# Four adaLN tiles behind each product weight, and the last silu ahead of the root, in a two-block Trainium2 kernel

## What is computed

```python
mod = silu(c) @ mod_w + mod_b                # shift, scale, gate
h = rmsnorm(x, norm_g) * (1 + scale) + shift
cv, cg, cs, lx, ls = split(h @ w_in)         # five parts of 1024
v = conv31(cv * sigmoid(cg)); v = silu(layernorm(v)) @ pw2_w + pw2_b
y_conv = v * silu(cs)
xs = conv4(lx)                               # 8 heads of 128
r = sigmoid(xs @ wr + br); i = sigmoid(xs @ wi + bi)
a = exp(-8 * r * softplus(-lam)); bx = sqrt(1 - a**2) * i * xs
y_lru = scan(a, bx) * silu(ls)
x = x + (1 + gate) * (concat(y_conv, y_lru) @ w_out)
# second block: adaLN from silu(c_2) @ ada_w_2 and silu(c_ctx_2) @ ada_w_2,
# then an mLSTM mixer and a convolutional FFN
```

## Time and profile before

| | |
|---|---|
| median of 3 runs | 2344.55 us (2343.93 to 2348.63) |
| the profiled execution | 2347.46 us |
| its span, first to last instruction | 2345.6 us |
| mean granted TensorE clock | 0.951 |
| PE busy | 2157.1 us, 92% |
| DVE busy | 1103.7 us, 47% |
| ACT busy | 774.6 us, 33% |
| POOL busy | 671.8 us, 29% |

### The profile page before, as it was taken

One profiled execution on the slowest core, in us unless ns is written; L12 is line 12 of the kernel. 1 busy time (PEld: TensorE's weight loads), 2 busy tenths in 40 slices (PEclk: granted clock), 3 DMA queues, 4 the chain that ended last, 5 costly groups with the idle time before them and its releaser, 6 DMA issues.

```text
span 2345.6 us, 26000 instructions
## 1 busy us (share of the span) xinstructions
PE 2157.1 (92%) x9876; PEld 1785.9 (76%) x9876; DVE 1103.7 (47%) x1039; ACT 774.6 (33%) x884; POOL 671.8 (29%) x308
## 2 busy tenths in 40 slices
PE   5999799997999999999979957979999999999995
PEld 4788687876878787888859946747888888887874
DVE  7689988777333656412236652082222222412124
ACT  4333254564342332122334443232222222302122
POOL 1466455544222221211201124402222222222240
PEclk7999999999999999999989977979999999999997
DMA  9431111221212333356578852121112122123211
GB/s 364 169 128 45 30 59 60 64 68 45 72 59 79 123 90 120 104 172 212 171 200 235 224 200 85 54 72 54 45 45 80 57 77 80 54 72 117 67 59 72
DMA packets 280109, 245.19 MB, mean 105 GB/s; under 512 B 7714, under 2 KB 251523, under 8 KB 280035
## 3 DMA queue, kind: packets, MB, share of 16 engines
q1 hardware_dynamic: 270355, 234.75, 32.5%
q10 hardware_dynamic: 9680, 9.44, 1.2%
HBM read 196.12 MB, written 48.04 MB: 104 GB/s over the span
## 4 chain that ended last, share of the span: by engine, by line
PE 41%; issue 38%; DVE 10%; POOL 6%; DMA 3%; ACT 2%; SPq 0%; POOLq 0%; ACTq 0%; DVEq 0%
PE PS L1372 31%; POOL wl L678 5%; DVE PS L1835 5%; PE PS L1641 1%; PE PS L1649 1%; PE PS L1642 1%; PE PS L1675 1%; PE PS L1528 1%; DVE SCR L1749 1%; DMA B<-rows_d 1%; PE PS L1615 1%; DMA SCR<-in_ctx 1%; PE PS L1635 1%; PE PS L1621 1%; PE PS L1634 1%
## 5 line engine op out<-in xcount | busy, mean ns | idle before, releaser
L1372 PE MATMUL PS<-XH,wh 128*128 128x512 f32 x2448 | 762.9, 393 | 28.9 <-POOL wl L678 18.3
L678 POOL TENSOR_TENSOR wl<-raw,wh 128x1024 fp32r<-128x1024 f32 (+2 forms) x177 | 415.6, 2348 | 1248.0 <-ACT wh L865 1026.1
L1372 PE MATMUL PS<-XL,wh 128*128 128x512 f32 x2448 | 759.1, 391 | 0.0
L1372 PE MATMUL PS<-XH,wl 128*128 128x512 f32 x2448 | 758.4, 391 | 0.0
L1372 PEld LDWEIGHTS PS<-XH,wh 128*128 128x128 f32 x2448 | 460.9, 189 | 133.3 <-POOL wl L678 16.3
L1372 PEld LDWEIGHTS PS<-XL,wh 128*128 128x128 f32 x2448 | 462.5, 189 | 96.9
L1372 PEld LDWEIGHTS PS<-XH,wl 128*128 128x128 f32 x2448 | 462.4, 189 | 96.9
L1835 DVE SCALAR_TENSOR_TENSOR PS<-B,PJ,PS 128x1022 f32<-128x1022 f32 (+7 forms) x197 | 251.1, 1274 | 7.5
L865 ACT ACTIVATE wh<-raw 128x1024 fp32r<-128x1024 f32 (+1 forms) x120 | 125.4, 1045 | 312.4 <-PE PS L1372 245.8
L2246 DVE SCALAR_TENSOR_TENSOR SCR<-SCR,PV 128x1008 f32<-128x1008 f32 x22 | 28.0, 1271 | 256.6 <-ACT SCR L1308 256.6
L939 ACT ACTIVATE wh<-raw 128x1024 fp32r<-128x1024 f32 (+1 forms) x56 | 54.1, 965 | 268.5 <-PE PS L1372 232.8
(11 more groups left out here) (337 smaller groups left out, 2440.7 us busy)
## 6 DMA issues: line engine op xcount, KB each, us to landing
B<-in_ada_w SPq DMA_DIRECT2D x48, 512.0 KB, 6.0
raw<-in_ffn_up_w SPq DMA_DIRECT2D x44, 512.0 KB, 4.1
raw<-in_w_in SPq DMA_DIRECT2D x40, 512.0 KB, 3.8
raw<-in_m_in_w SPq DMA_DIRECT2D x29, 512.0 KB, 5.2
proj_d<-B SPq DMA_DIRECT2D x17, 512.0 KB, 3.0
mod_tiles<-in_mod_w SPq DMA_DIRECT2D x16, 512.0 KB, 13.0
raw<-in_w_out SPq DMA_DIRECT2D x16, 512.0 KB, 4.3
B<-proj_d SPq DMA_DIRECT2D x8, 1024.0 KB, 6.5
```

Of the source, the lines that this page charges most:

```text
L678: tt(wl[slot][:, 0:kc, :], raw[slot][:, 0:kc, :], wh[slot][:, 0:kc, :].bitcast(F32), ALU.subtract).then_inc(lo_done, 1)
L1372: last = mm(ps[:, c:c + step_n], W[:, k, :], Y[:, k, c:c + step_n], start=(seen == 0), stop=(seen == total - 1))
```

## The change

SyncE's loop of the first pass loads four adaLN tiles behind each unit of weights from unit 4 on, not three: 3 to 6 behind unit 4, and so on to 19 to 22 behind unit 8 and tile 23 behind unit 9. On ScalarE, for the last head, a silu of one column (`spare` from `eps`) is added behind the copy of line 1050, and `ls_evac` of the last head goes ahead of the cast of G1's second unit, of three high halves and of the root. Its former place, between the high halves of blocks 6 and 7, is empty. All else is as before.

```diff
         eps = sb("eps", [P, 1])
+        spare = sb("spare", [P, 1])
...
             for U in range(4, 2 * KD):
                 l1_load(U)
-                for n in range(3 * (U - 3), min(3 * (U - 2), (1 + EARLY) * KD)):
+                for n in range(3 + 4 * (U - 4), min(3 + 4 * (U - 3), (1 + EARLY) * KD)):
                     ada_load(n)
...
                 f(r_t, r_t, ACT.Copy, bias=1.0).then_inc(ev("th_ok"), 1)
                 if last:
+                    f(spare[:], eps[:], ACT.Silu)
+                    ls_evac(i)
                     hi(ls_unit(i) + 2)
                     for k in range(DVE_HIGH, KD - 2):
                         lru_high(k)
...
             lru_high(KD - 2)
-            ls_evac(KD - 1)
             lru_high(KD - 1)
```

## The result

Five executions of the changed kernel gave a median of **2334.15 us** (2332.66 to 2335.51), beside 2346.96 us (2343.93 to 2348.63) for five of the kernel before: ratio **0.9948, 95% interval 0.9934 to 0.9963** (8.7 to 15.5 us). It is faster by 12.8 us where 21.2 were forecast, and its time lies above the forecast range. The profiled execution took 2335.51 us with a span of 2333.7. The changed kernel has one line more from line 171 on, up to three more near line 1053 and two behind it: 939 and 995 are now 940 and 996, the root of 1056 is 1059, and 1372, 1499, 1528, 1829 and 1852 are 1374, 1501, 1530, 1831 and 1854.

A forecast was written before the change was run, and what follows sets the result against it. TensorE, busy 92% of the span, bounds the kernel; two waits, 11.7 and 10.2 us, can be removed. Gains of 13.7 + 7.5 = 21.2 us take 2347.46 to 2326.3, median 2323.4; range 2320 to 2329.

The forecast's parts named there:

- the second part: ScalarE's last silu ahead of the root lets TensorE start G1 near 558.6, not 567.06, ending its opening 7.5 us earlier.
- Block 6: In G1's opening, its low half is ready at 570.3; ten TensorE blocks, 13.7 us, then end at 584.0.
- block 7's later root: In G1's opening, block ready at 576.1, TensorE comes at 578.5: the delay costs nothing, 2.4 us of cover.
- the Trainium skill's drain: On ScalarE, about 1.38 us more per table switch, 2.66 in all; would cut 1.4 us, but not charged.
- The adaLN sums: On VectorE, last sum ends at 140.0 instead of 151.99, set by tile 23's late load; VectorE gains 12.0 us.
- part 1: Four adaLN tiles behind each weight: gate products of head 0 end 14.5 us earlier, 0.8 given back, worth 13.7 us.
- The first taps: VectorE's four first conv taps before the short conv, 9.2 us in all, taken as unchanged; bounds 4.0 earlier, 3.9 later.
- the margin: At head 0's gate products, xs's low half is ready at 280.8, TensorE arrives at 281.17: 0.4 us to spare.
- part 1 falls short: Rival: bad tap collisions or slower landings leave 1 to 3.5 us of wait at the gates; 2324.4 to 2327, chance 0.12.
- half clock in the sparse stretch: Rival: TensorE's clock falls inside G1's opening, 556.9 to 571.7, costing 2.4 us; 2325.8, chance 0.12.
- Both gains stay: Behind G1's opening, all is set by TensorE's products and what follows them, so the full 21.2 us reaches the end.
- The base: Profiled execution of the kernel before, 2347.46 us, lies 2.9 above the median of three runs; 2326.3 becomes 2323.4.

The follow-up runs named there:

- f4_noload: The changed kernel without the added one-column silu, so the table load stands at the real silu: 2333.81 us, ratio 0.9936 to the kernel before.
- f1_after: The changed kernel run again, unaltered, beside the kernel before on another chip: 2333.95 us, ratio 0.9932.
- g3_after: The changed kernel run again, unaltered, as control for later runs: 16.9 us faster than the kernel before.
- e3_spare: The kernel before with the 128 x 1 tile allotted in SBUF and used by nothing: 2350.24 us, ratio 0.9996.
- e1_part1: The kernel before with only the four adaLN tiles behind each weight: 2339.27 us, ratio 0.995.
- The fills: Three runs of the changed kernel with two never-read TensorE products in each of three stalls, or only the first two: mean 2331.6 us over 15 executions.
- e4_nospare: The changed kernel without the new tile, its small silu writing a column of an unused existing tile: 2333.51 us, ratio 0.9918 to the kernel before.
- g1_all4: The changed kernel with all 21 remaining adaLN tiles sent behind unit 4: 2365.52 us, ratio 1.0072 to the kernel before.
- e2_part2: The kernel before with only the ScalarE change, the last head's silu ahead of the root: 2342.93 us, ratio 0.9961.

## Why the prediction was right or wrong

**What bounded the kernel, and the second part: right.** Block 6 was the limit, ten blocks behind it took 13.90 us (13.7 forecast), block 7's later root was covered. Worth 7.3 us between the marks and 7.7 us in time (7.5 forecast). The table load was 1.28 us with 0.02 behind it, and the root followed its load at once; the Trainium skill's drain ("ScalarE: Activation LUTs", What ACT_TABLE_LOAD costs) did not show here either. The step that hoisted it is worth nothing, though, as f4_noload shows.

**The adaLN sums: right.** The weights of unit 9 went out at 131.67, the last sum ended at 139.2 (140.0 forecast; 139.2 to 140.7 over the six traces with part 1 alone or with both, unfilled), no wait for weights appeared near 120 to 140. The wait of 11.7 us is gone. The first taps took 6.8 us in place of 9.2, inside the bounds; so the low half was ready at 278.05 or, in f1_after, at 279.00, where 280.8 was forecast, and the margin was 1.7 us in f1_after and up to 4.2 in others, not 0.4.

**Part 1's size: wrong.** The failed step is "the gate products end at 281.17 + 12 x 0.229 = 283.9, instead of at 298.46: 14.5 us". 283.9 is right for an execution in which TensorE meets no half-clock stretch near 248 (f1_after 283.67, g3_after 283.73). The step took both of its ends from one execution of the kernel before, as if fixed, while a wait of 11.7 us made the variation of TensorE's arrival invisible. Over the unfilled traces the mark is at 297.5 on average without part 1 (four, 295.4 to 298.6) and at 285.3 with it (six, 283.7 to 286.7): 12.2 us. Of the 2.3 us short, 1.4 are the arrival: 1.1 for a stretch near 248 in four of six, 0.3 for a later start of unit 16. The other 1.0 (all rounded) is that 298.46 was itself late: in e3_spare, for one, the four first taps took 6.7 us in place of 9.2, the low half ended at 290.01 and the mark came at 295.43. From there to head 7's gates part 1 loses 1.5 more on average (247.25 to 248.71; 0.8 forecast), of which 1.3 to 1.4 shows in traces without a stretch near 531 and 1.1 at the next head alone: the wait of 1.22 us for the weights' low half, where the forecast had read a head with one of 0.96. That leaves 10.7 us where 13.7 were forecast; e1_part1's time says 11.4. The rival "part 1 falls short" had about this size, but put it down to late taps and landings and a wait that remains, and none remained. The rival "half clock in the sparse stretch" expected the loss inside G1's opening, where half clock turned out to be free once the silu had moved. The forecast's ground against it, that a gap of 2.2 us is short, did not hold: stalls of 2.1 to 2.3 us were followed by half clock, though not in every execution.

**"Both gains stay": right, within 1 us.** From the opening to the end it is 1756.4 us on average in the three traces of the kernel before or with the spare tile alone (1754.0 to 1758.0), and 1757.2 in the five of the changed kernel and its variants without part of the silu or the tile (1754.9 to 1760.1). The traces with one part alone have 1756.6 and 1760.9. The two groups differ by less than each spreads, so 18.0 us at the opening become about 17.2 at the end. Theory C, a stage behind G1 bound by transfers that swallows a third of the gain, is out. Comparing the first two traces alone would have misled: there the stage takes 6.1 us more in the changed kernel.

**The base: wrong, and the largest part of the miss.** "That execution lies 2.9 us above the median of the three runs, so the median goes to 2323.4", with "some 2 us for the runs' own spread". The three were low. Single executions of the kernel before lie between 2343.9 and 2355.8, and the 48 of the four comparisons have a mean of 2350.0, 2.5 us above even the profiled one. The 16 of the changed kernel have a mean of 2332.8. So, with all executions taken together, the miss of 10.7 us comes apart as: 5.4 for the base (2350.0 - 2344.55), 4.0 for the gain (21.2 - 17.2: 3.0 of part 1, 0.2 of part 2, 0.8 downstream), and 1.3 because these five executions lie above that mean. The gains of 16.5 and 16.9 us in the later comparisons agree with 17.2; the first, 12.8, has an interval that ends at 15.5. Its five executions of the kernel before have a mean of 2346.4, the other three groups 2351.0, 2350.6 and 2348.9, each on another chip. Whether the first group was low by chance or by its occasion no run decides.

What also stays open: why the 3.4 us stretches come in some executions and not in others with the same stall. The fills don't settle whether the stalls bring them.

## What to carry to other kernels

A wait hides the variation of what arrives at it. Before costing its removal by the arrival time in one trace, ask how far that arrival moves from one execution to the next, since after the change it goes straight to the end. Take the base from as many executions as there are, and when a gain of 1% is at stake, put the spread of single executions (here 12 us) into the range in full. Moving work ahead in a queue pays up to the point where a batch outlasts the prefetch behind it: here four tiles per weight gave 11 us, and all at once lost 17.

## What was not expected of the hardware

A stall of 2.1 to 2.3 us of TensorE was followed by 3.4 us at 1.2 GHz in some executions and by none in others of the same kernel, at the same place and with the same program around it (248.01 in the changed kernel with 1.19 us for two products, 248.01 in g3_after with 0.70). Ahead of G1's opening the stalls were not all alike: 1.9 to 2.2 us in the changed kernel, e4_nospare and g1_all4, which have a stretch behind them, 1.6 to 1.7 in e2_part2, f1_after, f4_noload and g3_after, which have none. A table load did not wait for the product that its own silu reads: it started at 545.10 in f4_noload, the product ended at 545.97 and the silu started at 546.40, so hoisting the load by hand gained nothing.
